# Stick-breaking attention: value products directly ahead of the scores, cumulative products in the middle of the step, and the rounding of a weight tile in another step

## What is computed

```python
q, k, v, gate = jnp.split(h @ w_in, 4, axis=-1)        # 16 heads of 64
q = rms_norm(q, q_norm_g); k = rms_norm(k, k_norm_g)
z = jnp.einsum('bqhd,bshd->bhqs', q_blk, k) * scale
mask = key_pos[None, :] < q_pos[:, None]
log1m = jnp.where(mask, -jax.nn.softplus(z), 0.0)
after = lax.cumsum(log1m, axis=3, reverse=True) - log1m
wts = jnp.where(mask, jnp.exp(jax.nn.log_sigmoid(z) + after), 0.0)
o = jnp.einsum('bhqs,bshd->bqhd', wts, v)
return (o * jax.nn.silu(gate)) @ w_out
```

## Time and profile before

| | |
|---|---|
| time, median of 3 runs | 1773.86 us (1773.39 to 1777.37) |
| the profiled execution's own time | 1774.74 us |
| its span in the profile | 1772.9 us |
| tensor engine, matmul busy | 1739.5 us (98%) |
| tensor engine, weight load busy | 1419.5 us (80%) |
| VectorE, ScalarE, GpSimd busy | 889.4, 824.4, 664.8 us |
| the eight pairs of heads, first scores to last value product | 577.8 to 770.9 us |

### The profile page before, as it was taken

The page is one execution under the profiler, slowest core; times in us unless marked ns, Lnnn a source line. Parts: engine busy times, 40 slices in busy tenths (PEclk is TensorE's granted clock), DMA queues, the critical chain, the costliest instruction groups (busy, mean ns, idle before and its releaser), DMA issues.

```text
span 1772.9 us, 22596 instructions
## 1 busy us (share of the span) xinstructions
PE 1739.5 (98%) x8776; PEld 1419.5 (80%) x8776; DVE 889.4 (50%) x1326; ACT 824.4 (47%) x1191; POOL 664.8 (37%) x241
## 2 busy tenths in 40 slices
PE   7999999999999999999999999999999999999999
PEld 5688799888898666678788888888877888998887
DVE  6765954453132677744743333431177568435510
ACT  5575343685233767744422222222266734348720
POOL 1333420344425555444344444444334234014443
PEclk9999999999999999999999999999999999999999
DMA  4223210222222011112222222222222232012222
GB/s 175 95 72 96 72 42 7 96 96 95 95 95 87 33 48 48 47 54 100 86 97 100 101 103 97 95 95 95 83 92 75 72 96 84 14 48 95 95 95 71
DMA packets 48776, 143.70 MB, mean 81 GB/s; under 512 B 28080, under 2 KB 30256, under 8 KB 32816
## 3 DMA queue, kind: packets, MB, share of 16 engines
q1 hardware_dynamic: 48688, 142.50, 23.5%
HBM read 137.25 MB, written 5.24 MB: 80 GB/s over the span
## 4 chain that ended last, share of the span: by engine, by line
PE 74%; issue 17%; POOL 4%; ACT 2%; DVE 2%; DMA 0%; POOLq 0%; SPq 0%; ACTq 0%; DVEq 0%
PE ps L1648 19%; PE ps L1650 18%; PE ps L1649 18%; POOL w_lo L463 4%; PE ps L1913 3%; PE ps L1974 2%; PE ps L1940 2%; PE ps L2103 1%; PE ps L1960 1%; PE ps L1924 1%; PE ps L1969 1%; PE ps L2149 1%; PE ps L2047 1%; PE ps L2049 1%; PE ps L2048 1%
## 5 line engine op out<-in xcount | busy, mean ns | idle before, releaser
L463 POOL TENSOR_TENSOR w_lo<-w_raw,w_hi 128x2048 fp32r<-128x2048 f32 x107 | 505.5, 4724 | 796.1 <-ACT w_hi L595 792.9
L1648 PE MATMUL ps<-h_hi,w_hi 128*128 128x512 f32 x1488 | 596.7, 401 | 24.3 <-DVE w_lo L1028 10.0
L1650 PE MATMUL ps<-h_hi,w_lo 128*128 128x512 f32 x1488 | 582.0, 391 | 0.0
L1649 PE MATMUL ps<-h_lo,w_hi 128*128 128x512 f32 x1488 | 581.2, 391 | 0.0
L1648 PEld LDWEIGHTS ps<-h_hi,w_hi 128*128 128x128 f32 x1488 | 280.6, 189 | 103.2 <-issue 25.7
L1650 PEld LDWEIGHTS ps<-h_hi,w_lo 128*128 128x128 f32 x1488 | 280.3, 188 | 60.0
L1649 PEld LDWEIGHTS ps<-h_lo,w_hi 128*128 128x128 f32 x1488 | 280.9, 189 | 56.1 <-issue 1.4
L595 ACT ACTIVATE w_hi<-w_raw 128x2048 fp32r<-128x2048 f32 (+1 forms) x126 | 238.7, 1894 | 129.3 <-PE ps L1650 123.8
L1648 PE MATMUL ps<-y_hi,w_hi 128*128 128x512 f32 x448 | 174.3, 389 | 0.0
L1649 PE MATMUL ps<-y_lo,w_hi 128*128 128x512 f32 x448 | 174.3, 389 | 0.0
L1650 PE MATMUL ps<-y_hi,w_lo 128*128 128x512 f32 x448 | 174.3, 389 | 0.0
(11 more groups left out here) (209 smaller groups left out, 2344.2 us busy)
## 6 DMA issues: line engine op xcount, KB each, us to landing
w_raw<-w_tiles SPq DMA_DIRECT2D x124, 1024.0 KB, 4.9
x<-x_t SPq DMA_DIRECT2D x4, 512.0 KB, 6.9
out_t<-x SPq DMA_DIRECT2D x8, 256.0 KB, 5.7
w_raw<-w_tiles SPq DMA_DIRECT2D x2, 512.0 KB, 5.1
scr_u<-lt SPq DMA_DIRECT2D x8, 128.0 KB, 2.7
u_blk<-scr_u SPq DMA_DIRECT2D x2, 512.0 KB, 3.2
scr_t<-v_t SPq DMA_DIRECT2D x2, 512.0 KB, 2.6
scr_v<-v_blk SPq DMA_DIRECT2D x2, 512.0 KB, 3.3
```

Of the source, the lines that this page charges most:

```text
L463: pool.tensor_tensor(w_lo[:, slot, :], w_raw[:, slot, :], w_hi[:, slot, :].bitcast(F32), ALU.subtract).then_inc(lo_done, 1)
L1648: pe.matmul(out_, w_h, m_h, start=start, stop=False)
L1649: pe.matmul(out_, w_h, m_l, start=False, stop=False)
L1650: return pe.matmul(out_, w_l, m_h, start=False, stop=stop)
```

## The change

`pv(g-2)` is written ahead of `z(g)` instead of behind the first two blocks of the step. `cum(g-1)` follows the first two blocks (one in the last pair), and two blocks (one in the last pair) follow it, where it was three ahead and one behind. The number of blocks in a step stays. On ScalarE the rounding that stood in step 2 of pair j stands in step 0 of pair j+1, between the logarithms of `softplus(g)` and `square_qk` and `weights(g-1)`; it is the same tile. The last pair's own rounding in step 3 stays.

```diff
@@ stickbreak on ScalarE
                     softplus(g, j + 1 if more and v == 3 else None)
+                    if v == 0 and j:
+                        hi(t0 + 6 + j)
                     if more and v == 0:
                         square_qk(j + 1, 0)
                     if more and v == 1:
                         rms_qk(j + 1, 0)
                     if g:
                         weights(g - 1)
-                    if v == (2 if more else 3):
+                    if v == 3 and not more:
                         hi(t0 + 7 + j)
@@ stickbreak on the tensor engine
                 for v in range(4):
                     g = 4 * j + v
+                    if g >= 2:
+                        pv(g - 2)
                     z(g)
                     if more and v == 3:
                         sums(j + 1, 1)
                     fill(2 if more else 1)
                     if more and v == 1:
                         sums(j + 1, 0)
-                    if g >= 2:
-                        pv(g - 2)
-                    fill(1 if more else 0)
                     if g:
                         cum(g - 1)
-                    fill(1)
+                    fill(2 if more else 1)
```

## The result

The changed kernel takes 1778.28 us (median of 9 runs, 1778.1 to 1780.2); the kernel before, in the same sessions, 1773.55 us. The forecast median was 1780.1 us, in a range from 1775.5 to 1785.5.

A forecast was written before the change was run, and what follows sets the result against it. Bound by two close limits, the tensor engine's own work and a scores-ScalarE-weights ring. Six steady pairs +3.8, first pair +1.0, last +1.4 gave +6.2 on 1774.74, less 0.9: median 1780.1 us, range 1775.5 to 1785.5.

The forecast's parts named there:

- The ring: Scores, ScalarE's work, previous step's weights, next scores; the change adds a whole value product, 0.37 to 1.01 us by width.
- Step 3: Last step of a steady pair, scores of step 3 to next step 0: 7.25 us against 6.70, +0.55.
- steps 1 and 2 together: Middle steps of a steady pair: 10.91 us against 11.19, -0.28.
- The gap between value and score products: Tensor engine's gap from value product to scores, taken as 0.16 us; bounds 0 and 0.32 move the sum -3 to +4.
- Step 0: First step of a steady pair, with the moved rounding between logarithms and weights: 6.52 us against 6.15, +0.37.
- The ends: First and last pair of the stretch: +1.0 us for the first, +1.4 us for the last (14.37 against 12.95).
- The split in halves: Of the 6.2 us lost, about half from the value product in the ring, the other half from the rounding.
- The fast one: Rival: tensor engine is the bound, joined value products and scores save 0.19 us a step; 1768.1 or less; chance 0.08.
- The "no change" case: Rival: earlier cumulative products or hidden rounding cancel the loss, leaving some 3 us, 1777; chance 0.27.
- the case of the sum: The whole kernel's time as worked out, 1777.5 to 1783 us; chance 0.55.
- the slow one: Rival: gap to score products at its upper bound, or VectorE's parts late for cumulative products; 1784 to 1786; chance 0.10.
- The signs: Profile marks: value products idle 0.4 to 0.8 us for weights, no wait at scores, steady pairs 24.6 to 24.7.

The follow-up runs named there:

- the two-buffer runs: Changed kernel's order, rounding in step 2, second weight buffer, value products a step earlier; cumulative products behind two or three blocks; against the kernel before: 1770.32 and 1770.2 us.
- `a_pe_order_only`: The tensor engine's new order alone, rounding left in step 2, against the kernel before: ratio 1.0018, +3.2 us.
- `d_rounding_behind_weights`: The changed kernel with the rounding in step 0 behind the weights instead of ahead of them; against the kernel before: ratio 1.0019, +3.4 us.
- `e_sums_middle_only`: The kernel before with only the cumulative products moved one block earlier: ratio 1.0 (0.9991 to 1.0009).
- the second-buffer-alone kernel: The kernel before with a second buffer for the weights and nothing moved: ratio 0.9998 (0.9989 to 1.0007).
- `c_values_behind_scores`: The changed kernel with the value products directly behind the scores instead of ahead of them; against the kernel before: ratio 1.0006, +1.1 us.

## Why the prediction was right, point by point

**The ring.** Shown. The value product ahead of the scores, waiting for the same weights, is the larger part of the loss: exchanging the two takes 3.40 of the stage's 4.68 back, and when the value products wait for nothing, the same adjacency becomes a gain. Step 3 came out at 7.25 to the hundredth, and steps 1 and 2 together at 10.91 (688.78 - 677.87) for 10.91.

**The gap between value and score products.** Taken as 0.16 between bounds of 0 and 0.32; measured 0.15 to 0.16 at all four widths. The drain rule cited from the Trainium skill (TensorEngine Tiling (Array Packing), Key Properties) agrees with the two-buffer runs, in which one change of mode fewer a step gave back 0.2. It could not decide the time here, since the engine was waiting anyway.

**Step 0, the term that was mis-sized.** Forecast 6.52, measured 677.87 - 671.58 = 6.29. The working let the second absolute value wait for VectorE's sum of step 3, 1.07 behind the scores. In the profile after, both absolute values stand in one record at 672.27, 0.69 behind the scores, with a wait for the mask and none for VectorE. The step of the prediction that failed is "that chain hangs on step 3's scores: 648.35 + 24.04 - 663.91 = 8.48". Carried over, it put the second absolute value 8.32 behind step 3's scores. Now VectorE's second sum ends 7.68 behind them (671.33 + 0.68 - 664.33), ahead of the mask. VectorE's chain was held in the kernel before by one slow instruction, and that instruction is no longer slow. VectorE in step 3 of the changed kernel, ahead of the scores at 671.58:

```profile
667.93 0.76 DVE L1490 SCALAR_TENSOR_TENSOR sb_qk<-sb_raw,par,sb_r 128x512 f32<-128x512 f32 x1 [0.47 <-ACT sb_r L882]
669.49 0.69 DVE L1508 SCALAR_TENSOR_TENSOR sb_sp<-ps,sb_t 128x512 f32<-128x512 f32 x1 [0.80 <-ACT sb_t L899]
```

and the same step of the kernel before, ahead of the scores at 670.61:

```profile
667.66 2.26 DVE L1488 SCALAR_TENSOR_TENSOR sb_qk<-sb_raw,par,sb_r 128x512 f32<-128x512 f32 x1 [0.90 <-ACT sb_r L882]
669.84 0.68 DVE L1506 SCALAR_TENSOR_TENSOR sb_sp<-ps,sb_t 128x512 f32<-128x512 f32 x1
```

The same scaling of the keys takes 0.76 where it took 2.26. So the sum no longer stood in line behind it but waited for ScalarE's logarithm. The term was too high by 0.23 in five of the six pairs, by 0.05 in the sixth (the one of 24.63) and by 0.22 in the last pair: 1.4 of the 1.5 us by which the sum was too high.

**The ends.** First pair 21.61 against 20.62 (598.45 - 577.83), +0.99 for a forecast +1.0. Last pair 29.26 against 28.13, +1.13 for +1.4; its step 0 was 5.76 and not 5.98, the same VectorE term, and its steps 1 and 2 were 3.54 and 4.82 for 3.60 and 4.79.

**The split in halves.** Roughly so, by the stage: the order alone +2.36, the rounding alone +1.13, both together +4.68. In the new order the rounding costs 2.3, twice what it costs in the old one. The difference is not in step 0, nor in the last pair: there the move costs about 0.2 a pair and 1.0 in either order. It is in step 3. In the old order the rounding in step 2 was in the way of step 3, as the prediction found (0.16), and moving it gives back 0.13 in each steady pair and 0.27 in the first. In the new order it was in nobody's way there: step 3 takes 7.25 with the rounding in step 2 and with the rounding in step 0, so the move gives nothing back. The prediction's reason for the other half holds: without the rounding, step 0 is bound by the tensor engine (6.11, no wait at the value products).

**The rivals.** The fast one had its size right (0.19 a step, found as 0.20 to 0.21) and its condition wrong, as argued: it needs weights that are ready. The "no change" case was right about its size, not about its cause: the measured 4.7 lies under 5.3 by a mis-sized term, not because the effects cancel. By the prediction's own line the result thus falls where it had put 0.30, and not where it had put 0.63; the direction, the range and the case of the sum (1777.5 to 1783) held. In the slow one, neither the gap nor late sums appeared.

**The signs.** No wait was left at the scores, and ScalarE's weights follow without idle time, as named. Steady pairs came out at 24.45 for the named 24.6 to 24.7, and step 0 at 6.29 for "near 6.5", both by the term above. The idle times ahead of the value products were named as 0.4 to 0.8; in the steady pairs they run from 0.36 to 1.11.

## What to carry to other kernels

Before moving an instruction ahead of another that waits for the same event, ask whether the second one starts the next round of a dependency ring. If it does, everything put ahead of it is paid in full, and what it saves on its own engine is not seen. Place behind the wait's first user what the ring does not need, or take the moved work from a round earlier, which costs a buffer. With the rounding left in step 2, the same adjacency lengthened the stage by 2.4 us in the first form and shortened it by 5.0 us in the second. And when work is moved out of one wait into another, count both ends: the same move cost twice as much in the new order, because there the place that it left had nothing to give back.

## What was not expected of the hardware

**VectorE and GpSimd at the same time.** The same 128x512 instruction took 0.76 us and 2.26 us. In the changed kernel GpSimd began its own 128x768 subtraction at 668.22, 0.29 us behind VectorE's start:

```profile
668.22 2.18 POOL L511 TENSOR_TENSOR run_lo<-run,run_hi 128x768 fp32r<-128x768 f32 x1
```

In the kernel before, GpSimd's instruction of the same kind lay from 643.46 to 645.31 and VectorE's, from 643.62, ended only at 645.86, just behind it. In the changed kernel VectorE started first and was done in 0.76, and GpSimd's took 2.18 where it had taken 1.85. The ten profiles have six such pairs of instructions each, from the second pair of heads on, and they fall into two groups. Where VectorE began 0.29 to 0.45 ahead of GpSimd (the changed kernel, `a_pe_order_only`, `d_rounding_behind_weights` and the two with value products of a step earlier), its instruction took 0.75 to 0.92 and GpSimd's 2.16 to 2.18. Where VectorE began behind GpSimd or no more than 0.04 ahead (the other five), it took 2.20 to 2.43, and GpSimd's 1.84 to 1.86. It looks as if the two hinder each other and as if a start of a few hundredths ahead is not enough to win. No run isolates it, so the cause stays an argument; that the durations go with these starts in all 60 cases is shown.

**Two short stretches at the lower clock.** The stage of `e_sums_middle_only` is 1.18 us shorter, its time the same; the two-buffer kernels gain 5.0 and 5.2 in the stage and 3.7 and 3.8 in the medians; and the span of the second-buffer-alone kernel is 1.6 us above that of the kernel before, with the same stage. The granted clock shows where profiles differ. This is the second-buffer-alone kernel, and then the changed kernel, in windows shortly after the next layer begins (columns: window, its length, then busy time and count of PE, PEld, DVE, ACT and POOL, granted clock, DMA share, GB/s):

```profile
868.00:890.00 22.00, 19.83 (x81) 15.98 (x81) 18.97 (x17) 7.24 (x7) 9.21 (x2) 0.92 0.23 80
```

```profile
868.00:890.00 22.00, 19.83 (x88) 16.11 (x87) 19.57 (x19) 9.02 (x10) 8.97 (x2) 1.00 0.18 70
```

In the first the clock is at its lower level, 1.2 of 2.4 GHz, for a part of the window (0.52 of full speed from 880 to 882), and 7 multiplications fewer get done, which at 0.23 each is the 1.6 us. A wait of the tensor engine of about 2.2 us falls into this window in both (19.83 busy of 22). The kernel before has the same wait and full clock behind it. `e_sums_middle_only` and both kernels with value products of a step earlier have 0.92 in this window too, so their profiles give back 1.6 there. But so has `c_values_behind_scores`, whose time and stage agree; one profile for each kernel doesn't show how often its runs meet this stretch, and so how much of a median it explains stays open. Another such stretch lies ahead of the first scores:

```profile
566.00:572.00 6.00, 3.22 (x8) 2.58 (x9) 2.67 (x1) 3.26 (x4) 5.84 (x3) 0.66 0.00 0
```

This row is of the second-buffer-alone kernel; in the changed kernel the same window has 0.84, and its scores begin 1.2 us earlier than those of the kernel before, with the same code up to there. In this window the tensor engine was idle for about half of the time. Over the ten profiles the first scores start between 575.55 and 578.37. So one profile's span cannot be compared with another's to better than 2 to 3 us here, and the length of the stage between two marks is the sharper measure of a change inside it.
